# The gate's silu in the two last mixer stages: a tanh on ScalarE and one product on VectorE in place of ScalarE's silu

## The reference

```
for l in range(DEPTH):                       # DEPTH = 2
    h = x * (1.0 + scale) + shift
    (p_cq, p_ckv, p_kr, p_qb, p_kb, p_vb, p_qc, p_kc, p_vc,
     p_qi, p_ki, p_wi, p_gate) = jnp.split(h @ w_in[l], SPLIT_POINTS, axis=-1)
    o_a = mla_attention(...)                 # 6 heads, columns 0 to 383
    o_b = dilated_attention(...)             # 6 heads, columns 384 to 767
    o_c = sparse_attention(...)              # 4 heads, columns 768 to 1023
    y = jnp.concatenate([o_a, o_b, o_c], axis=-1) * jax.nn.silu(p_gate)
    sub = y @ w_out[l]
    x = layer_norm_2(ALPHA * x + (1.0 + gate) * sub, ln_g[l], ln_b[l])
```

## Time and profile before

| | us |
|---|---|
| median of three runs | 1333.62 |
| lowest, highest | 1332.83, 1333.98 |
| the profiled execution, its own time | 1334.87 |
| its span in the profile | 1333.1 |
| PE busy | 1312.4 (98%) |
| DVE busy | 1024.9 (77%) |
| ACT busy | 675.0 (51%) |

### The profile page before, as it was taken

One profiled execution on the slowest core, in us unless ns is written; L12 is line 12 of the kernel. 1 busy time (PEld: TensorE's weight loads), 2 busy tenths in 40 slices (PEclk: granted clock), 3 DMA queues, 4 the chain that ended last, 5 costly groups with the idle time before them and its releaser, 6 DMA issues.

```text
span 1333.1 us, 18844 instructions
## 1 busy us (share of the span) xinstructions
PE 1312.4 (98%) x7096; PEld 1110.5 (83%) x7096; DVE 1024.9 (77%) x1625; ACT 675.0 (51%) x1069; POOL 105.4 (8%) x153
## 2 busy tenths in 40 slices
PE   9999999999999999999999999999999999999997
PEld 7888888788888888888887888888889998798995
DVE  6677778887777677777687887778777789966897
ACT  6444445644444444444446535444435758447572
POOL 1011000011011001110010011111000000000000
PEclk9999999999999999999999999999999999999999
DMA  8977756438777656776646348776656463464630
GB/s 273 320 231 227 233 181 210 136 96 262 236 234 230 206 189 229 223 238 224 223 159 212 109 153 306 233 259 225 206 166 199 136 221 127 143 213 130 190 127 32
DMA packets 195049, 264.92 MB, mean 199 GB/s; under 512 B 17232, under 2 KB 140240, under 8 KB 194448
## 3 DMA queue, kind: packets, MB, share of 16 engines
q1 hardware_dynamic: 183248, 223.12, 52.1%
q0 software_dynamic: 11712, 40.60, 8.8%
HBM read 262.61 MB, written 1.07 MB: 198 GB/s over the span
## 4 chain that ended last, share of the span: by engine, by line
PE 80%; DVE 11%; ACT 4%; DMA 3%; issue 2%; SPq 0%; DVEq 0%; ACTq 0%
PE ps L812 24%; PE ps L814 24%; PE ps L813 24%; PE ps L896 4%; DVE w_lo L1311 3%; DMA w_raw<-in_ffn_w_gu 2%; ACT w_hi L1135 1%; ACT att L1245 1%; DVE att L1496 1%; PE ps L1104 1%; DVE arena L1603 1%; PE ps L1043 1%; DVE small L1601 1%; DVE few_first L1506 1%; DVE few_first L1340 1%
## 5 line engine op out<-in xcount | busy, mean ns | idle before, releaser
L1311 DVE TENSOR_TENSOR w_lo<-w_raw,w_hi 128x1024 fp32r<-128x1024 f32 (+2 forms) x420 | 497.2, 1215 | 134.8 <-ACT w_hi L1135 132.3
L1135 ACT ACTIVATE w_hi<-w_raw 128x1024 fp32r<-128x1024 f32 (+2 forms) x420 | 431.1, 1053 | 248.2 <-DMA w_raw<-in_ffn_w_gu 127.4
L812 PE MATMUL ps<-w_hi,col_hi 128*128 128x512 f32 (+2 forms) x1024 | 396.6, 387 | 3.2 <-DVE w_lo L1311 1.5
L814 PE MATMUL ps<-w_hi,col_lo 128*128 128x512 f32 (+2 forms) x1024 | 392.1, 383 | 0.0
L813 PE MATMUL ps<-w_lo,col_hi 128*128 128x512 f32 (+2 forms) x1024 | 391.8, 383 | 0.0
L812 PEld LDWEIGHTS ps<-w_hi,col_hi 128*128 128x128 f32 x1024 | 192.5, 188 | 43.4 <-DVE w_lo L1311 4.1
L814 PEld LDWEIGHTS ps<-w_hi,col_lo 128*128 128x128 f32 x1024 | 192.4, 188 | 38.0
L813 PEld LDWEIGHTS ps<-w_lo,col_hi 128*128 128x128 f32 x1024 | 192.7, 188 | 34.9
L812 PE MATMUL ps<-w_hi,lat_hi 128*128 128x512 f32 (+2 forms) x544 | 208.9, 384 | 0.0
L814 PE MATMUL ps<-w_hi,lat_lo 128*128 128x512 f32 (+2 forms) x544 | 206.5, 380 | 0.0
L813 PE MATMUL ps<-w_lo,lat_hi 128*128 128x512 f32 (+2 forms) x544 | 206.3, 379 | 0.0
(11 more groups left out here) (148 smaller groups left out, 1175.8 us busy)
## 6 DMA issues: line engine op xcount, KB each, us to landing
w_raw<-in_ffn_w_gu SPq DMA_DIRECT2D x352, 256.0 KB, 4.5
w_raw<-in_w_in SPq DMA_DIRECT2D x108, 512.0 KB, 4.6
w_raw<-in_ffn_w_down SPq DMA_DIRECT2D x88, 512.0 KB, 4.9
mod<-in_w_ada POOLq DMA_DIRECT2D x32, 768.0 KB, 7.8
w_raw<-in_w_out SPq DMA_DIRECT2D x24, 512.0 KB, 4.5
norm_g<-in_ln_g POOLq DMA_DIRECT2D x8, 512.0 KB, 4.1
norm_b<-in_ln_b POOLq DMA_DIRECT2D x8, 512.0 KB, 5.7
w_raw<-in_w_out SPq DMA_DIRECT2D x16, 256.0 KB, 4.5
```

The costliest lines, as they stand in the source:

```text
L812: pe.matmul(dst, a_hi, b_hi, start=start, stop=False)
L814: return pe.matmul(dst, a_lo, b_hi, start=False, stop=stop)
L1135: act.activation(half_of(w_hi[j], n, h), half_of(raw[j], n, h), ACT.Copy).then_inc(hi_ready, 1)
L1311: tt(half_of(w_lo[j], n, h), half_of(raw[j], n, h), half_of(w_hi[j], n, h).bitcast(F32), ALU.subtract)\
```

## The change

ACT now writes tanh(g/2) to `gate_t`. A new job `gatecol:q` on DVE takes the place of the other half of the function: it reads `gate_t` and the same PSUM bank and writes (tanh + 1) times g back to `gate_t`. The factor 0.5 that is left goes into the `gate` job, which becomes a `scalar_tensor_tensor` with 0.5. Whoever waited for the gate's silu, `gate` and PE's next use of the bank, now waits for `gatecol` (`gated`). Four `gatecol` jobs stand in the order of each of stages 6 and 7.

```
-mix:A:0 lo:G/3:0 hi:out/1:0 turn:A:1 score:C:0 lo:G/3:1 ...
+mix:A:0 lo:G/3:0 gatecol:0 hi:out/1:0 turn:A:1 score:C:0 lo:G/3:1 ...
+score:C:1 gatecol:1 lo:out/0:0 mix:A:2 gate:1:0 weigh:C:1 ...
+T:G:2 T:G:3 gatecol:2 gate:0:1 mix:C:0 gate:1:1 gatecol:3 turn:C:1 +modload +fold ...
...
+                    elif got[1][0] == "G":
+                        COUNT.add("curved", group)
+                        COUNT.add("gated", group)
+                        held[bank] = ("gated", COUNT.value["gated", group])
...
-                    pe.wait_ge({"hidden": hidden_done, "copied": copied}[name], value)
+                    pe.wait_ge({"hidden": hidden_done, "copied": copied, "gated": gated}[name], value)
...
-                    dst, func = (gate_t, ACT.Silu) if name[0] == "G" else (cols2, ACT.Copy)
-                    act.activation(dst[:, first:first + tiles, :],
-                                   bank(b, tiles * S).rearrange("p (t n) -> p t n", t=tiles), func).then_inc(copied, 1)
+                    src = bank(b, tiles * S).rearrange("p (t n) -> p t n", t=tiles)
+                    if name[0] == "G":
+                        act.activation(gate_t[:, first:first + tiles, :], src, ACT.Tanh, scale=0.5).then_inc(curved, 1)
+                    else:
+                        act.activation(cols2[:, first:first + tiles, :], src, ACT.Copy).then_inc(copied, 1)
...
+                elif kind == "gatecol":
+                    name = ("G", job[2])
+                    b, first, tiles = TURNED[name]
+                    dve.wait_ge(curved, at["curved", (s, name, None)])
+                    cols = gate_t[:, first:first + tiles, :]
+                    stt(cols, cols, 1.0, bank(b, tiles * S).rearrange("p (t n) -> p t n", t=tiles), ALU.add, ALU.mult)\
+                        .then_inc(gated, 1)
...
-                    dve.wait_ge(copied, max(at["copied", (s, ("G", k // 2), None)] for k in tiles))
-                    tt(v, v, gate_t[:, tiles[0]:tiles[-1] + 1, i * P:(i + 1) * P], ALU.mult).then_inc(y_ready, 1)
+                    dve.wait_ge(gated, max(at["gated", (s, ("G", k // 2), None)] for k in tiles))
+                    stt(v, v, 0.5, gate_t[:, tiles[0]:tiles[-1] + 1, i * P:(i + 1) * P], ALU.mult, ALU.mult).then_inc(y_ready, 1)
```

More of the change, by code:

```diff
@@ L236 @@
 hi:G/3:1 T:QC:1 hi:out/0:0 turn:A:0 weigh:A:1 score:A:2 lo:G/1:0 lo:G/1:1 lo:G/2:0 hi:out/0:1 lo:G/2:1 T:G:0
-mix:A:0 lo:G/3:0 hi:out/1:0 turn:A:1 score:C:0 lo:G/3:1 weigh:A:2 weigh:C:0 T:G:1 mix:A:1 turn:A:2 topk:1:3
-score:C:1 lo:out/0:0 mix:A:2 gate:1:0 weigh:C:1 gate:0:0 lo:out/0:1 lo:out/1:0 hi:out/1:1 turn:C:0 ycols:0:0
-T:G:2 T:G:3 gate:0:1 mix:C:0 gate:1:1 turn:C:1 +modload +fold gate:0:2 hi:out/2:0 ycols:1:0 ycols:1:1 mix:C:1
+mix:A:0 lo:G/3:0 gatecol:0 hi:out/1:0 turn:A:1 score:C:0 lo:G/3:1 weigh:A:2 weigh:C:0 T:G:1 mix:A:1 turn:A:2 topk:1:3
+score:C:1 gatecol:1 lo:out/0:0 mix:A:2 gate:1:0 weigh:C:1 gate:0:0 lo:out/0:1 lo:out/1:0 hi:out/1:1 turn:C:0 ycols:0:0
+T:G:2 T:G:3 gatecol:2 gate:0:1 mix:C:0 gate:1:1 gatecol:3 turn:C:1 +modload +fold gate:0:2 hi:out/2:0 ycols:1:0 ycols:1:1 mix:C:1
 ycols:0:1 ycols:0:2 lo:out/1:1 lo:out/2:0 lo:out/2:1 lo:out/3:0 hi:out/2:1 hi:out/3:0 out:0:0 gate:1:2 hi:out/3:1
@@ L704, in build @@
          weighed, y_cols, ret_mixed, half_sum, var_ready, rstd_ready, h_ready, x_ready, y_ready, rope_done, rotated, idx_w_ready,
-         idx_summed, rope_a_done, rope_k_done, squares, latent, folded, mod_summed, mod_hi, mod_lo, mod_row) = (
+         idx_summed, rope_a_done, rope_k_done, squares, latent, folded, mod_summed, mod_hi, mod_lo, mod_row, curved, gated) = (
             sem(n) for n in ("group_done", "silu_done", "hidden_done", "copied", "hi_part", "scores", "score_free", "maxed",
@@ L708, in build @@
                              "h_ready", "x_ready", "y_ready", "rope_done", "rotated", "idx_w_ready", "idx_summed",
-                             "rope_a_done", "rope_k_done", "squares", "latent", "folded", "mod_summed", "mod_hi", "mod_lo", "mod_row"))
+                             "rope_a_done", "rope_k_done", "squares", "latent", "folded", "mod_summed", "mod_hi", "mod_lo", "mod_row",
+                             "gate_curved", "gate_ready"))
         x_in = [[sem(f"x_landed{i}{h}") for h in range(2)] for i in range(TT)]
```

## The result

| | before | after |
|---|---|---|
| median of 22 runs each, us | 1333.86 | 1336.32 |
| lowest, highest | 1332.70, 1336.39 | 1334.58, 1339.57 |
| ratio of after to before | | 1.0020, 95% interval 1.0014 to 1.0026 |
| the profiled execution, its span | 1334.87, 1333.1 | 1335.19, 1333.4 |

The change makes the kernel 2.5 us slower. The runs after are spread wider than those before: eleven lie at 1334.6 to 1336.1, eleven at 1336.5 and above, three of these over 1339. Two things turn out to lie behind the spread, and only one of them comes from the change.

What follows compares the result with a forecast made beforehand. PE was busy 98%, with DVE setting the end of stage 6's last 45 us and PE right behind. Stage 6 +1.9 and stage 7 +0.1 gave +2.0 on 1333.62, so 1335.6 us; range 1332.5 to 1338.0.

Steps and rivals of the forecast that it cites:

- the likeliest case: Whole kernel: stage 6 +1.9 us, stage 7 +0.1, so 1335.6 us; own range 1334.9 to 1336.6, chance 0.57.
- The eleven loads are worth 0.41 us twice: Stages 6 and 7: removing ACT's table loads can give only PE's 0.41 us idle before `mix:A:2`, twice, 0.8 us.
- The 0.41 us at `mix:A:2` are lost to DVE through `gatecol:0`: Both stages: `gatecol:0` adds 0.60 us on DVE, `turn:A:2` starts 0.5 later, `mix:A:2` ends up +0.1 per stage.
- `gatecol:1` is hidden: Behind the maximum of `score:C:1`: it falls into DVE's 1.39 us idle, with 0.4 us left before `T:G:3`.
- 1.9 us on DVE's unbroken stretch reach `out:1:0` and `xt:0:0`: Stage 6: `gatecol:0`, `:2` and `:3` add 0.60, 0.72 and 0.60, making `ycols`, `out:1:0` and `xt:0:0` 1.9 us later.
- In stage 7 they are hidden, 0.3 us left over: Before stage 7's `ycols`: 1.9 us of `gatecol` work falls into DVE's 2.21 us idle, with 0.3 us over.
- The first rival: DVE pays in both stages because the hidden parts aren't hidden: 1.9 + 1.9 = +3.8 us, 1337.4; chance 0.18.
- the second: Three loads ahead of `turn:A:2` are on the path in both stages: 7.7 us less, 1325.9; chance 0.06.
- The third: DVE's chain in stage 6 has unseen slack, so the 0.41 us is won twice: 1332.8; chance 0.09.
- the fourth: Half of DVE's 1.9 us is given back in stage 7 or at the fold: +1.0 or less, 1334; chance 0.10.
- the start of `out:1:0` 2 us late: Expected in the profile after: in stage 6 `out:1:0` starts about 2 us behind the matmul before it.
- a stretch below the granted clock: Sign of being wrong in the profile after: a stretch of PE below the granted clock all slices have now.

Runs made afterwards that it cites:

- the gain alone: The change with the tanh but no `gatecol` jobs, leaving out the 1 and the factor g: 1333.03 us, ratio 0.9992 against the kernel before.
- the costs alone: The change with ACT's silu kept, so all table loads and the eight `gatecol` are there: 1336.34 us, ratio 1.0016 against the kernel before.

## Why the prediction was right, and what it lacked

The forecast was 1335.6 us and +2.0; the median moved by 2.5 to 1336.3, inside the likeliest case's own range. The forecast had the change within 0.2%, and the ratio, 1.0020, lies on that border. The mechanism was right: stage 6 moved by 1.98 us where 1.9 was foreseen, for the reason that was given. That the median also came within 0.5 us is in part luck, since two things that were not in the sum work against each other in it: a loss of clock in some runs, and, in the profiles at least, an earlier arrival at stage 6.

- *The eleven loads are worth 0.41 us twice.* Too high by some 0.3 us: the run with the gain alone got nothing in stage 6 and 0.5 us in stage 7.
- *The 0.41 us at `mix:A:2` are lost to DVE through `gatecol:0`.* Right: `turn:A:2` waits 0.38 us (0.4 to 0.5 foreseen). From `mix:A:0` to `mix:A:2` it is 11.54 us after and 11.58 before: -0.04 instead of +0.1.
- *`gatecol:1` is hidden.* Right: 0.6 us less of DVE's idle, and no idle before `T:G:3`.
- *1.9 us on DVE's unbroken stretch reach `out:1:0` and `xt:0:0`.* Right: 1.98 in three profiles, 0.60 + 0.79 + 0.60.
- *In stage 7 they are hidden, 0.3 us left over.* Right, with 0.16 left. The margin was over-stated: in stage 7, without `fold` between, the next instruction needs the result of `gatecol:3` too, so both cost 0.78, where the sum had 0.72 and 0.60.
- *The first rival* (paid in stage 7 too) and *the second* (7.7 us faster) are out: stage 7 has not moved, and the gain without the costs measured 1.1 us faster, not 7.7. *The third* (0.41 us won twice) and *the fourth* (half of the 1.9 given back) are out by the stages: stage 6 takes 1.98 more, and from `xt:0:0` to the end nothing comes back.
- *Missing from the sum: what 2 us of idle do to PE's clock.* The prediction named the start of `out:1:0` 2 us late and, as a sign of being wrong, a stretch below the granted clock, but didn't join the two. The idle costs its own length in every execution and another 1.3 to 1.5 us in some, 1.1 of it in stage 6. This is shown for one of the change's four profiles.

What stays open: how many of the change's executions lose the clock, and where its highest runs (1339.1 to 1339.6, over 4 us above 1335) lose more than the one profile did; their mean clock of 0.996 and 0.997 points to the clock, but no such run was profiled. Nor is it settled why the change's `mix:A:0` came at 1099.5 to 1099.9 in four profiles and that of before at 1099.8 to 1101.4 in three. Four other kernels with the same instructions ahead came at 1100.1 to 1101.1 (the costs alone, the gain alone, `gatecol:0` later, `fold` behind the `ycols`), three of them with the eight `gatecol`, so these do not make it early; chance is the likelier reading, and not shown.

## What to carry to other kernels

Removing work from an engine that nobody waits for buys nothing: read how long the busiest engine idles behind it, and which engine would end the next wait; here 14 us of table loads stood against 0.8 us of idle, and of 5 us of new work on DVE the 2 us that lay on its unbroken stretch were paid in full. Before you add work to an engine, look for the place in its queue where it idles and put it ahead of that; `gatecol:1`, and `gatecol:2` and `gatecol:3` in stage 7, cost nothing for this reason. `gatecol:0` stood where DVE was not idle, and took back in stage 7 what the loads had given. And where a forecast makes a short idle of PE several times longer, price what the clock may do behind it, and profile more than once: one execution may show none of it. A wait that is removed can also come back at once behind its place: count a gain only at the end of the next stage.

## What the runs showed of the hardware

- The granted clock fell from 1.00 to 0.50 to 0.52 behind idles of PE of 1.96 us (one of four executions with this idle), 2.12 us and 2.90 us (the one profile of each), and in no profile behind 1.38 us. PE was busy without a gap behind the idle; the clock fell 0.2 to 1.2 us after PE had started again, and was back after about 3 to 4 us. The Trainium skill, page "TensorE: Matmul & The Clock Gate", section "Part 1: The HAM clock gate (the "warmup" mystery)", tells of the lower level after idle time; the trace agrees on the two levels, and shows that the same idle does it in one execution and not in the next.
- A table load costs 1.28 us and the next function starts 0.01 behind it. ACT's busy time fell by 15.1 us, 14.1 of it the eleven loads. The rest is an estimate: it is overlap, where no load lies between, an instruction starts about 0.1 us before the end of the one ahead (the tanh at 1101.28, ahead of it a copy from 1100.33 of 1.06 us), eleven times.
- GpSimd took 2.4 to 3.6 us for an elementwise operation on 128 x 1024 in the one profile that has it, where DVE takes 1.22. While it worked, a 128 x 128 operation of DVE took 0.69 instead of 0.23 and a 128 x 6 one 0.36 instead of 0.17 us, some 0.7 us in all over 12 us; that GpSimd was the cause is not shown.
- Executions differ by up to 1.9 us in when they reach stage 6 (1099.53 to 1101.41, with the same instructions ahead), while the stage itself repeats to 0.01 us where the clock holds: a change of this size is read from the stage, not from the span.
